# One encoder layer on one core: who sums the experts' rows, and how the last stage's gate and norm rows reach 128 partitions

## The reference

```python
x = x + gt1 * mixer_output(oa, ob, rb, g_head, w_out)
h = modulate(rmsnorm(x, g_ffn), sh2, sc2)
x = x + gt2 * moe_ffn(h, ...)      # 32 experts, each token goes to 2 of one group of 8
...
y_prompt = rmsnorm(xp, g_final)
y_sample = rmsnorm(xs, g_final)
```

## Time and profile before

| | |
|---|---|
| time, median of 3 runs | 1840.95 us (1836.69 to 1844.86) |
| profiled execution, its own time | 1836.31 us |
| its span, first to last instruction | 1834.7 us |
| PE, PEld, DVE, ACT, POOL busy | 85%, 43%, 22%, 11%, 9% |
| mean granted TensorE clock | 0.977 of full |
| DMA | 617.25 MB, mean 336 GB/s |

### The profile page before, as it was taken

One profiled execution on the slowest core, in us unless ns is written; L12 is line 12 of the kernel. 1 busy time (PEld: TensorE's weight loads), 2 busy tenths in 40 slices (PEclk: granted clock), 3 DMA queues, 4 the chain that ended last, 5 costly groups with the idle time before them and its releaser, 6 DMA issues. The chain is left out here.

```text
span 1834.7 us, 21697 instructions
## 1 busy us (share of the span) xinstructions
PE 1551.0 (85%) x8893; PEld 795.4 (43%) x8893; DVE 400.9 (22%) x878; ACT 196.5 (11%) x521; POOL 166.7 (9%) x360
## 2 busy tenths in 40 slices
PE   5999999999999999978988777777777777778773
PEld 2455454444454444555544343434343434334331
DVE  2012322224242220452111111111111111111117
ACT  3001111111211100110000000000000000000002
POOL 1031000000102020020101101010101010101000
PEclk9999999999999999979989999999999999999997
DMA  9998767656626584379999999999999999999992
GB/s 364 382 310 301 286 272 298 265 219 260 202 69 236 175 236 150 155 272 420 425 427 427 427 427 428 427 428 426 428 425 426 426 422 425 425 423 423 427 391 101
DMA packets 103622, 617.25 MB, mean 336 GB/s; under 512 B 15701, under 2 KB 17861, under 8 KB 67977
## 3 DMA queue, kind: packets, MB, share of 16 engines
q1 hardware_dynamic: 85922, 571.73, 76.8%
q0 software_dynamic: 17648, 44.79, 7.9%
HBM read 603.03 MB, written 34.16 MB: 347 GB/s over the span
## 5 line engine op out<-in xcount | busy, mean ns | idle before, releaser
L1298 PE MATMUL bank<-ring,zbuf 128*64 128x256 f32 x4096 | 469.8, 384 | 161.1 <-DMA ring<-in_w_expert_up 99.1
L1298 PEld LDWEIGHTS bank<-ring,zbuf 128*64 128x64 f32 x4096 | 287.3, 138 | 355.7 <-DMA ring<-in_w_expert_up 123.2
L1321 PE MATMUL bank<-ring,hbuf 128*64 128x512 f32 x1024 | 236.9, 607 | 32.5 <-ACT hbuf L1672 23.0
L861 PE MATMUL bank<-ring,hbuf 128*128 128x512 f32 x384 | 174.2, 599 | 3.0 <-ACT xbuf L1443 2.6
L1321 PEld LDWEIGHTS bank<-ring,hbuf 128*64 128x64 f32 x1024 | 70.6, 139 | 177.7 <-issue 121.2
L857 PE MATMUL bank<-hbuf,ring 128*128 128x384 f32 x384 | 133.8, 495 | 1.2 <-ACT zbuf L1439 0.8
L1161 PE MATMUL bank<-ring,zbuf 128*128 128x512 f32 x288 | 128.7, 602 | 3.1 <-DVE ring L1982 1.9
L861 PEld LDWEIGHTS bank<-ring,hbuf 128*128 128x128 f32 x384 | 70.2, 190 | 83.7 <-issue 82.7
L857 PEld LDWEIGHTS bank<-hbuf,ring 128*128 128x128 f32 x384 | 69.8, 190 | 52.5 <-issue 11.0
L1161 PEld LDWEIGHTS bank<-ring,zbuf 128*128 128x128 f32 x288 | 54.2, 192 | 69.9 <-issue 69.8
L682 POOL CAST cur<-stab 128x1 int32 (+1 forms) x31 | 6.3, 202 | 832.0 <-DVE zbuf L2168 832.0
(11 more groups left out here) (408 smaller groups left out, 1143.2 us busy)
## 6 DMA issues: line engine op xcount, KB each, us to landing
ring<-in_w_expert_up SPq DMA_DIRECT2D x64, 2048.0 KB, 26.9
ring<-in_w_expert_gate SPq DMA_DIRECT2D x64, 2048.0 KB, 26.8
ring<-in_w_expert_down SPq DMA_DIRECT2D x64, 2048.0 KB, 26.9
ring<-in_w_ada SPq DMA_DIRECT2D x96, 1024.0 KB, 8.1
ring<-in_w_in SPq DMA_DIRECT2D x32, 1024.0 KB, 9.2
ring<-in_w_out SPq DMA_DIRECT2D x16, 1024.0 KB, 5.1
y_rows<-modr POOLq DMA_DIRECT2D x1, 6144.0 KB, 22.6
ring<-y_rows SPq DMA_DIRECT2D x3, 2048.0 KB, 22.5
```

What stands on the lines that cost most here:

```text
L861: last = mm(bank[t][:, :], hT[:, k, t * P:(t + 1) * P], w[:, kk_, :], start=(k == 0), stop=(k == KC - 1))
L1298: last = mm(bank[2 + j // 4][64 * q:64 * q + 64, 0:256], xeT[u][:, k % 8, k // 8, :], w[:, kk_, 256 * q:256 * q + 256], start=(k == 0), st ...
L1321: last = mm(bank[5 + n][64 * q:64 * q + 64, :], hidT[u][:, k % 2, k // 2, :], unit(8 + k)[:, 1024 * q + QN * n:1024 * q + QN * n + QN], st ...
```

## The change

TensorE sums the expert rows of all three tiles as it did for t = 2 alone, and the gate rows and the final norm's weights are loaded once, into 10 partitions, and spread by products with a 0/1 matrix.

- POOL: the twelve loads go. After the last h2 store, before the first gather, two loads bring `mod_row`: the 9 gate rows (72 KB) and `g_final` (8 KB), one row on each of 10 partitions.
- DVE: three small copies make `pick_row` (10 x 384, a 0/1 matrix) between `normed_rows(1)` and `route(0)`.
- TensorE: after the router's last product and before `rows_T` of expert 0, 12 products of depth 10 and 512 columns, through banks 2 to 5 in turn; the fifth and later ones wait for the copy that frees their bank. ACT has 12 copies of 128x512 to `gbc` and `gfin`, ahead of its `rows_copy` of expert 0.
- End: `gated`, `early_sum`, `early_add`, `y_prompt` and `gate_half` go. Expert 31's outputs are copied once (DVE half, ACT half) to `ysb[1]`. For each tile TensorE waits for its rows and does the two products of depth 128 for each quarter and the one of depth 64. In t = 0 all eight of depth 128 come first, then the wait for `last_rdy`, then the four of depth 64. DVE multiplies and adds for all tiles. Order on DVE: add 0, add 1 (sum of squares 0 after its first quarter), norm 0, add 2 (sum 1 after its first quarter), norm 1, sum 2, norm 2.

```diff
@@ gpsimd
+            pool.wait_ge(x1, 6)
+            g.dma_start(mod_row[0:9, :], mod_dram[3, 0:9]).then_inc(gbc_in, 16)
+            g.dma_start(mod_row[9:10, :], A["g_final"].unsqueeze(0)).then_inc(gbc_in, 16)
             pool.wait_ge(unit_used, U_MOE)
...
-            spread_rows(gbc[:, 0, :], gbc[:, 1, :], 3, gbc_in)
-            for q in range(2):
-                g.dma_start(gate_half[64 * q:64 * q + 64, :],
-                            mod_dram[3, 0:1, 1024 * q:1024 * q + 1024].broadcast_to([64, 1024])).then_inc(gbc_in, 16)
-            pool.wait_ge(x1, 6)
-            g.dma_start(gfin, A["g_final"].unsqueeze(0).broadcast_to([P, D])).then_inc(gfin_in, 16)
@@ tensor
-            def back_to_tokens(t, n, b, more):
+            def early_rows(t, n, b):
+
+                for k in range(2):
+                    mm(bank[b][:, :], diag[:, k, t, :], yk[t][:, k, QN * n:QN * n + QN], start=(k == 0), stop=False)
+
+            def back_to_tokens(t, n, b, start):
...
+            pe.wait_ge(gbc_in, 32)
+            pe.wait_ge(pick_rdy, 1)
+            for m in range(12):
+                if m >= 4:
+                    pe.wait_ge(gates_sb, m - 3)
+                mm(bank[2 + m % 4][:, :], pick_row[:, m // 4, :], mod_row[:, QN * (m % 4):QN * (m % 4) + QN],
+                   start=True, stop=True).then_inc(rows_ps, 1)
             rows_T(0, 0, 16)
...
-            pe.wait_ge(last_rdy, 1)
             for t in range(NT):
-                if t == 2:
-                    pe.wait_ge(y2_rdy, 1)
+                pe.wait_ge(yk_in[t], 16)
                 for n in range(4):
                     if t == 2:
                         pe.wait_ge(fin_sum, n + 1)
-                    back_to_tokens(t, n, LATE_BANKS[t][n], t == 2).then_inc(late_ps, 1)
+                    early_rows(t, n, LATE_BANKS[t][n])
+                    if t:
+                        back_to_tokens(t, n, LATE_BANKS[t][n], False).then_inc(late_ps, 1)
+                if t == 0:
+                    pe.wait_ge(last_rdy, 1)
+                    for n in range(4):
+                        back_to_tokens(t, n, LATE_BANKS[t][n], False).then_inc(late_ps, 1)
@@ scalar
+            for m in range(12):
+                s, n = m // 4, m % 4
+                act.wait_ge(rows_ps, m + 1)
+                out = gfin if s == 2 else gbc[:, s, :]
+                cp(out[:, QN * n:QN * n + QN], bank[2 + n][:, :]).then_inc(gates_sb, 1)
             for t in range(NT):
                 act.wait_ge(h2_out[t], 16)
             rows_copy(0, 0)
@@ vector
+            cp(pick_row[:, 0, :], ident[0:10, 0:1].broadcast_to([10, P]))
+            cp(pick_row[:, 1, :].rearrange("p (b t) -> p b t", b=DEC_B), ident[0:10, 1:9].unsqueeze(2).broadcast_to([10, DEC_B, DEC_T]))
+            cp(pick_row[:, 2, :], ident[0:10, 9:10].broadcast_to([10, P])).then_inc(pick_rdy, 1)
             dve.wait_ge(router_in, 64)
...
-                tt(y_prompt[:, QN:2 * QN], bank[6][:, :], gate_half[:, QN:2 * QN], ALU.mult).then_inc(y_v, 1)
-                dve.wait_ge(y_a, NE + 2 * block)
-                tt(y_prompt[:, 0:QN], bank[5][:, :], gate_half[:, 0:QN], ALU.mult).then_inc(y_v, 1)
+                cp(ysb[1][:, 0:QN], bank[5][:, :]).then_inc(y_v, 1)
...
                 xs = x[:, t, QN * n:QN * n + QN]
-                if t < 2:
-                    return tt(xs, xs, bank[b][:, :], ALU.add)
-                chain(tt(late_tmp[n], bank[b][:, :], gbc[:, 1, QN * n:QN * n + QN], ALU.mult))
+                chain(tt(late_tmp[n], bank[b][:, :], gbc[:, t // 2, QN * n:QN * n + QN], ALU.mult))
                 return tt(xs, xs, late_tmp[n], ALU.add)
...
             add_late(0)
             add_late(1)
-            squares_sum(0)
-            squares_sum(1)
             normed(0)
+            add_late(2)
             normed(1)
-            add_late(2)
             squares_sum(2)
             normed(2)
```

More of the change, by code:

```diff
@@ L247, in encoder_step @@
         gfin = hbuf[:, 2048:4096]
-        gate_half = hbuf[:, 5120:6144]
+        mod_row = hbuf[0:10, 4096:6144]
+        pick_row = modr[0:10, 3, 0:384].rearrange("p (s n) -> p s n", s=3)
         iota_p = mods_free[:, 0:2 * TOK]
@@ L478, in _ @@
                 sp.wait_ge(last_rdy, 1)
-                rows_back(2)
-                sp.wait_ge(yk_in[2], 32)
+                sp.wait_ge(sct[0], 16 * 16)
+                sp.wait_ge(sct[1], 16 * 15)
+                for t in range(NT):
+                    rows_back(t)
             with sp.Else():
-                sp.nop()
-            sp.nop().then_inc(y2_rdy, 1)
+                for t in range(NT):
+                    sp.wait_ge(unit_used, U_MOE + UE * (NE - 1) + 2 * t + 2)
+                    if t == 0:
+                        sp.wait_ge(sct[0], 16 * 16)
+                        sp.wait_ge(sct[1], 16 * 15)
+                    rows_back(t)
             for t in range(NT):
@@ L1332, in gate_rows @@
                     last.then_inc(rows_ps, 1)
-            def back_to_tokens(t, n, b, more):
+            def early_rows(t, n, b):
+                for k in range(2):
+                    mm(bank[b][:, :], diag[:, k, t, :], yk[t][:, k, QN * n:QN * n + QN], start=(k == 0), stop=False)
+            def back_to_tokens(t, n, b, start):
                 r = slice(64 * (n // 2), 64 * (n // 2) + 64)
-                src = ysb[1] if t == 2 else y_prompt
-                if more:
-                    for k in range(2):
-                        mm(bank[b][:, :], diag[:, k, t, :], yk[t][:, k, QN * n:QN * n + QN], start=(k == 0), stop=False)
-                return mm(bank[b][:, :], hot[r, t * P:t * P + P], src[r, QN * (n % 2):QN * (n % 2) + QN],
-                          start=not more, stop=True)
+                return mm(bank[b][:, :], hot[r, t * P:t * P + P], ysb[1][r, QN * (n % 2):QN * (n % 2) + QN],
+                          start=start, stop=True)
+            pe.wait_ge(gbc_in, 32)
[5 more added lines that the diff above has]
+                   start=True, stop=True).then_inc(rows_ps, 1)
             rows_T(0, 0, 16)
@@ L1348, in two_experts @@
                     e = 2 * i + u
+                    if isinstance(i, int) and e == 0:
+                        pe.wait_ge(gates_sb, 12)
                     if isinstance(i, int) and e == 1:
-                        pe.wait_ge(gates_sb, 1)
+                        pe.wait_ge(gates_sb, 13)
                     up(u, e, e + 1)
@@ L1374, in _ @@
                     hidden_T(0, e)
-                    down(0, e, 2 * i + NE + 1)
+                    down(0, e, i + NE)
             with pe.Else():
                 pe.nop()
-            pe.wait_ge(last_rdy, 1)
             for t in range(NT):
-                if t == 2:
-                    pe.wait_ge(y2_rdy, 1)
+                pe.wait_ge(yk_in[t], 16)
                 for n in range(4):
@@ L1655, in _, with last_rows @@
             rows_copy(0, 0)
-            def gated(t):
-                act.wait_ge(yk_in[t], 16)
-                af(yk[t][:, 0, :], yk[t][:, 0, :], ACT.Copy, scale=gate[:, 0, t:t + 1]).then_inc(y_gated, 1)
-            def last_rows(e, block):
+            def last_rows(e):
                 act.wait_ge(unit_used, U_MOE + UE + e * UE)
-                cp(ysb[1][:, 0:QN], bank[5][:, :]).then_inc(y_a, 1)
-                act.wait_ge(y_v, NE + 2 * block)
                 cp(ysb[1][:, QN:2 * QN], bank[6][:, :]).then_inc(y_a, 1)
@@ L1715, in late_squares @@
                     af(sqf[:, 0:QN], x[:, t, QN * n:QN * n + QN], ACT.Square, accum_out=x1_parts[:, t, n:n + 1]).then_inc(x1sq, 1)
-            late_squares(0)
-            late_squares(1)
-            inv_rms(x1sum, 4, slice(0, 1), slice(0, 1), D)
-            inv_rms(x1sum, 5, slice(1, 2), slice(1, 2), D)
-            late_squares(2)
-            inv_rms(x1sum, 6, slice(2, 3), slice(2, 3), D)
+            for t in range(NT):
+                late_squares(t)
+                inv_rms(x1sum, t + 4, slice(t, t + 1), slice(t, t + 1), D)
         @block.vector
@@ L2319, in add_late @@
                     add_rows(t, n, LATE_BANKS[t][n], fin).then_inc(fin_sum, 1)
+                    if t and n == 0:
+                        squares_sum(t - 1)
             def squares_sum(t):
```

67 lines of the change are left out of this document (19 added, 48 removed).

## The result

The changed kernel takes 1842.6 us (median of 20 runs, 1841.2 to 1848.0); the kernel before, timed beside it, 1834.0 (20 runs, 1831.8 to 1844.9). The ratio is 1.0038, with a 95% interval from 1.0027 to 1.0048: slower by 0.38%, where I had forecast 0.42% less. The median of three that I had summed against, 1840.95, was 7 us high for this kernel; what counts is the ratio. The profiled execution took 1842.54 us with a span of 1841.0, against 1836.31 and 1834.7.

A forecast was written before the change was run, and what follows sets the result against it. The weight stream was taken to bound the expert loop. Head 6.3 us (3.4 + 2.9) and end 1.4 made 7.7 us off the median 1840.95, giving 1833.3; own range 1829 to 1838, 8 in 10 1825 to 1843.

The forecast's parts named there:

- What bounds the kernel: Expert loop: it runs at the pace of the weight stream, so only fewer bytes or an earlier stream start shorten it.
- Rival E: Loop: scatter, gather, transposes and products end it, not the stream; head's gain lost, 1.4 us stay, 1839.5; chance 0.08.
- The loads that go: Head of the loop: removing the gate and norm row loads ends a backlog, 3.4 us earlier (bounds 0 and 6).
- Rival B: Head of the loop: backlog 6 us instead of 3.4, rest as forecast; 10.3 us less, 1830.7; chance 0.16.
- The twelve products: Head, TensorE: products fit under the 6.87 us wait for the gather, costing 0; 1.6 us late if 0.7 each.
- rival C: Head: products stay at low clock, transposes start 3.8 us late, 2.9 lost, backlog still gone; 1840; chance 0.12.
- The clock: Head: products keep TensorE busy, full clock by 816.4; transposes 0.8 and `up` 2.1 us shorter, 2.9 together.
- The cover: Head, ACT: twelve copies at 0.55 us end at 817.1, ahead of expert 0's `rows_copy`; cover about 0.5 us.
- The data were there in time: Head: `mod_row`, 80 KB issued near 798, has 11 us until the products at 809.6, even behind the 1 MB store.
- The end: After the loop: ACT and DVE stall goes, TensorE's 33 us of products are late next; 1.4 us earlier.
- Rival A: End: TensorE overlaps the two shapes without drains, quarters 2.15 us; 14.2 us less in all, 1826.8; chance 0.07.
- Rival D: End: runs at the low clock after a gap over 3.3 us, 21.6 us later; 1854.9; chance 0.07.

The follow-up runs named there:

- e10: Kernel before with the new end in e8's order, old gate and norm loads kept, no depth-10 products; ratio to the kernel before 0.9967, median 1829.75 us.
- e3: Kernel before without the twelve gate and norm row loads and their waits, nothing in their place; median 1830.94 us, ratio to the kernel before 0.9984.
- e1: Changed kernel with only the new end: ten of the twelve old loads, no products, copies or `mod_row`; median 1835.67 us, ratio to the kernel before 1.0002.
- e11: e1 run once more, unchanged; 1833.53 us.
- e4: Changed kernel with the 12 products at depth 32 instead of 10; ratio to the kernel before 1.0051.
- e5: Changed kernel with the 12 products at depth 128 instead of 10; one execution 1830.75 us, the same kernel timed later at ratio 0.9987 to the kernel before.
- e9: e8 with the 12 products moved behind `up` of expert 1, inside the loop; median 1827.81 us, ratio to the kernel before 0.9950.
- e8: Changed kernel with products on four row groups, copies shared by ACT and DVE, end done tile by tile, depth 128 before depth 64; ratio to the kernel before 0.9958.

## Why the prediction was wrong, point by point

**What bounds the kernel: right.** In every kernel here, a shift of the first weight pair came through to the end. The stream takes 940.8 to 941.6 us in all kernels with the products and 942.6 to 944.4 in those with the loads (947.4 in the profiled execution of e10), and 942.4 in e3, which has neither, whenever it starts. Rival E is excluded.

**The loads that go, 3.4 us: right in kind, and the size fits.** The first pair lands after 7.8 us instead of 11.1, and the stream is 3.6 us shorter (2.0 in e3). That the size came out so close is partly luck, as the spread of e1, e10 and e11 shows. Rival B's 6 isn't seen.

**The twelve products at 0 us, bound 1.6: this step failed, and it alone turned the sign.** They took 20.84 us in a wait of 6.87, and the difference, 14.0, is the measured 13.8. The size came from the wrong row. I divided L1341's 5.81 us by eight products of depth 64, though there half of the products stand on the upper 64 of the array's rows and half on the lower 64 (`r` in `back_to_tokens`), and they run side by side: in the trace their records start in pairs, 0.01 to 0.08 us apart, the pairs 0.84 to 1.0 us apart at the low clock. The row that answers stood in the same group: four records of depth 128 in 1.95 us at the full clock, so some 0.43 a record, 0.86 a product, and twice that at the low clock. 12 x 1.72 is 20.6 us. e4 and e5 show that depth is no part of the price: 10 and 32 cost the same, and at 128 the records cost 0.85 as well until the clock rises. I had in fact used 0.86 in rival C, but as a price at the low clock. At 1.72 that rival comes to 809.6 + 20.6 = 830.2, 13.8 us after 816.4, and that was the result.

**The clock, 2.9 us: this step failed too.** I took an engine without a pause to be enough. It was at work for 20.84 us, and the granted clock stayed at 0.50; in e9 it even fell right after such products. With the same products at depth 128 the clock rose 4.4 us after the first, and the 2.9 us were there. "TensorE: Matmul & The Clock Gate" of the Trainium skill, Part 1, has the clock follow how busy the engine is; these rows disagree, if busy means an engine with an instruction at work. What Part 4 of that page of the Trainium skill says of transposes, that the full clock doesn't engage for them, is spoken against once more: in e5 eight transposes ran in 1.05 us behind the risen clock. Had I kept the clock term at 0 and the rest as it was, the forecast would have been 1836.2, still on the wrong side, so it is the smaller error.

**The cover.** The copies' pace, 0.58 us each, was right but never mattered. ACT waited for the products.

**The data were there in time: right.** L1346 starts at 806.87, as the router's product ends.

**The end, 1.4 us earlier: right.** It was 2.1. TensorE starts at the landing with the clock up, its quarters are 2.96, and DVE waits for it in add 1. Rival A isn't seen in the changed kernel. Its 2.15 us for a quarter put the product of depth 64 at 0.43, the same misreading as above; alone it costs 0.86. e8 comes near the 2.15 (8.98 / 4 = 2.25) by another order, and mostly because its products of depth 64 run two by two. Rival D's point, a pause over 3.3 us, was met in e1, e10 and e11 and not in the changed kernel, whose pause is 1.2 us. Its price was 1.7 to 3 us and not 21.6, because the clock comes back in the first products. (The 0.70 in 1789 to 1790 puts the fall in the kernel before at 1789.4, 3.0 us after TensorE's last product, where I had read 1789.7 and 3.3; nothing hung on it.)

The sum, put right: 3.4 + 1.4 earlier and 13.8 later is 9.0 later; from the rows of the changed kernel it is 13.8 + 0.6 - 3.6 - 2.1 = 8.7, and the timed medians differ by 8.6. I had also written that a change under 0.5% can't be told from none here; 20 runs of each told 0.38% from zero.

## What to carry to other kernels

Price a new product by the row that has its columns and its type at the clock that it will meet, and ask of each such row whether its products share the array; a quotient of a group's time is no price of one. Before a step is put into a wait, compare its dearest reading with the wait's length: here 20 us went into 7, while the same work a few steps later, in a stretch bound by the weight stream, cost nothing that the rows show (e9). Broadcasting rows by DMA can cost the transfers behind it more than its bytes say: at the loop's 427 GB/s these 3.67 MB would have been through in 8.6 us, well before 825, as they are issued from 811.8 on. What it is worth to remove such loads is small here, 2.9 us where nothing took their place (e3), and 1.9 where cheap products off the path did (medians of e9 and e10, on one chip, whose intervals overlap).

## What the runs showed of the hardware that I had not expected

- The granted clock stayed at its lower level, 0.50, through 20.8 us of unbroken f32 products of depth 10 or 32, and rose to the higher one 4.4 us into the same products at depth 128. In e9 it fell from 1.00 to 0.50 right after products of depth 10 that had TensorE at work for 4.9 of 5.7 us. Whether the array rows in use matter or the data in them (the added rows of `mod_row` held leftovers, those of `pick_row` zeros) wasn't told apart.
- A product of 512 f32 columns costs 1.7 us at the low clock, whether it is 10, 32 or 128 deep, and some 0.86 at depth 128 at the high one. Four products of depth 10 on four row groups cost 2.09 and 1.14 together. "TensorEngine Tiling (Array Packing)" of the Trainium skill describes such row groups ("Available Configurations"), and the rows agree that they run side by side.
- A single product of depth 64 between two of depth 128 costs 1.05 us, and four in a row on two row groups 1.99. "Mode switching requires drain", says that same page of the Trainium skill ("Key Properties"). The rows agree that a change of shape costs something, but not much: about 0.19 us at the full clock. Six changes fewer are 1.2 of the 2.9 us that e8 saves in each of tiles 1 and 2; the other 1.7 are the products that run side by side.
- In the two programs with the old loads and the new end (e1 and e11, e10) TensorE started 2.1 to 2.3 us after the landing that released it, in three executions of three, with nothing in the timeline that it waited for, and a 16 KB transfer of instructions under way beside it. Whether the one comes of the other isn't shown.
